# Two-layer streaming encoder on one core: gate products in one block for each attention unit, of 24, 24, 12 and 12 matmuls in turn

## What is computed

```python
z = x @ w_in[l]                      # -> q_A, k_A, v_A, c_q, c_kv, k_rope
y_a = swa(...)                       # mixer A: banded attention, 8 heads of 64, window 128, sinks, bias
y_b = mla(...)                       # mixer B: latent attention, 8 heads, over 512 rows or a cache of 512 + 16
g = sigmoid(x @ w_gate + b_gate)     # 1024 -> 2048: the gate products
h = g[:, :D] * (y_a @ w_proj_a) + g[:, D:] * (y_b @ w_proj_b)
x = LN1(alpha * x + h @ w_out)
x = LN2(alpha * x + ConvGLU(x))
```

## Time and profile before

| | |
|---|---|
| median of 3 runs | 1992.0 us (1989.5 to 1996.69) |
| the profiled execution | 1990.17 us, its span 1988.4 us |
| TensorE busy (matmuls) | 1896.4 us, 95% |
| weight loads on TensorE | 1790.4 us, 90% |
| DVE, ACT, GpSimd busy | 51%, 34%, 28% |
| mean granted clock of TensorE | 0.982 of full speed |
| instructions in the profile | 32255 |
| attention of layer 0, from the first gate matmul to the last values | 151.8 to 390.4 us |
| attention of layer 1 | from 1131.4 us |

### The profile page before, as it was taken

How to read it: one execution, slowest core, us unless ns; L and a number is a source line. 1 busy time by engine, 2 the same in 40 slices (tenths; PEclk the granted TensorE clock), 3 DMA queues, 4 the chain that set the end, 5 groups by cost and what they waited for, 6 DMA issues and landing times.

```text
span 1988.4 us, 32255 instructions
## 1 busy us (share of the span) xinstructions
PE 1896.4 (95%) x12626; PEld 1790.4 (90%) x12626; DVE 1023.7 (51%) x1589; ACT 667.6 (34%) x1372; POOL 566.3 (28%) x252
## 2 busy tenths in 40 slices
PE   7988999999999999999999889999999999999996
PEld 6876788799899999999988778888998999999996
DVE  3457534447764432443664674445587543334447
ACT  2224333442454312332231343334334442123323
POOL 2421111124143234332322211111332432443331
PEclk9999999999999999999989999999999999999998
DMA  6333222242122122221231412323321221222111
GB/s 176 114 87 116 78 81 98 73 151 86 43 85 84 57 70 94 75 69 53 80 119 54 146 42 90 102 78 110 123 79 43 86 78 64 70 97 72 61 59 65
DMA packets 58800, 169.41 MB, mean 85 GB/s; under 512 B 8120, under 2 KB 26216, under 8 KB 50728
## 3 DMA queue, kind: packets, MB, share of 16 engines
q1 hardware_dynamic: 58696, 167.97, 25.2%
HBM read 149.42 MB, written 18.28 MB: 84 GB/s over the span
## 4 chain that ended last, share of the span: by engine, by line
PE 83%; DVE 6%; issue 4%; ACT 2%; DMA 2%; POOL 2%; SPq 1%; POOLq 0%; ACTq 0%; DVEq 0%
PE ps L1429 58%; PE ps L1661 9%; PE ps L1736 3%; PE ps L1459 2%; PE ps L1587 2%; POOL w_lo L617 2%; PE ps L1564 2%; ACT probs L711 1%; PE ps L1634 1%; PE ps L1573 1%; DVE rms L995 1%; DVE probs L1095 1%; DVE st_mx L1066 1%; DVE probs L1065 1%; PE ps L1571 1%
## 5 line engine op out<-in xcount | busy, mean ns | idle before, releaser
L617 POOL TENSOR_TENSOR w_lo<-w_raw,w_hi 128x1024 fp32r<-128x1024 f32 (+3 forms) x248 | 566.1, 2291 | 1387.1 <-ACT w_hi L668 1376.4
L668 ACT ACTIVATE w_hi<-w_raw 128x1024 fp32r<-128x1024 f32 (+3 forms) x244 | 231.2, 968 | 416.5 <-PE ps L1429 398.2
L1429 PE MATMUL ps<-x_hi,w_hi 128*128 128x320 f32 x1504 | 346.1, 311 | 13.3 <-POOL w_lo L617 13.3
L1429 PE MATMUL ps<-x_lo,w_hi 128*128 128x320 f32 x1504 | 345.0, 311 | 0.0
L1429 PE MATMUL ps<-x_hi,w_lo 128*128 128x320 f32 x1504 | 344.8, 311 | 0.0
L1429 PEld LDWEIGHTS ps<-x_hi,w_hi 128*128 128x128 f32 x1504 | 253.6, 189 | 15.0 <-issue 5.9
L1429 PEld LDWEIGHTS ps<-x_lo,w_hi 128*128 128x128 f32 x1504 | 253.9, 189 | 0.0
L1429 PEld LDWEIGHTS ps<-x_hi,w_lo 128*128 128x128 f32 x1504 | 253.6, 189 | 0.0
L1661 PE MATMUL ps<-x_hi,w_hi 128*128 128x320 f32 x512 | 173.8, 339 | 8.5 <-ACT logits L744 8.3
L1334 DVE TENSOR_SCALAR f_conv<-f_ext,vec 128x656 f32<-128x656 f32 x44 | 67.3, 1529 | 211.1 <-ACT tail L879 209.5
L1661 PE MATMUL ps<-x_hi,w_lo 128*128 128x320 f32 x512 | 159.6, 312 | 0.0
(11 more groups left out here) (238 smaller groups left out, 3173.0 us busy)
## 6 DMA issues: line engine op xcount, KB each, us to landing
w_raw<-in_slabs SPq DMA_DIRECT2D x86, 1024.0 KB, 4.8
w_raw<-in_slabs SPq DMA_DIRECT2D x20, 768.0 KB, 4.0
gate_logits<-logits SPq DMA_DIRECT2D x64, 160.0 KB, 1.8
gates<-gate_logits SPq DMA_DIRECT2D x16, 640.0 KB, 6.5
w_raw<-in_slabs SPq DMA_DIRECT2D x16, 640.0 KB, 3.7
ckvc<-in_ckvc SPq DMA_DIRECT2D x16, 256.0 KB, 2.9
ckvc_t<-in_ckvc_t SPq DMA_DIRECT2D x16, 256.0 KB, 3.0
x_in<-in_x_t SPq DMA_DIRECT2D x4, 640.0 KB, 8.7
```

The lines of the kernel that those rows point to most:

```text
L617: pool.tensor_tensor(w_lo[:, s % 2, c], w_raw[:, s % 2, c], w_hi[:, s % 2, c].bitcast(F32), ALU.subtract).then_inc(wlo_ready, 1)
L668: A(w_hi[:, s % 2, c], w_raw[:, s % 2, c], ACT.Copy).then_inc(whi_ready, 1)
L1429: ins = MM(out_[:, a, :], w, x[:, t, a * HT:(a + 1) * HT], start=t == 0 and w is wh and x is hi, stop=t == tiles - 1 and w is wl)
```

## The change

The gate products of a unit are no longer spread over three places. Behind scores(u+2) and ahead of values(u) stands one block: two halves (24 matmuls, one whole product) in units 0 and 1 of every four, one half (12 matmuls) in units 2 and 3. The number of matmuls is the same, and so is that of halves before units 0, 4, 8 and so on. ACT's `take_gate` always stands behind exps(u+2). `quarter_at_scores` follows the new counts: 48, 54, 64, 72, 80, 90, 100, 108 for the eight caches, before 48, 54, 64, 72, 82, 90, 100, 108.

```diff
 NG = 4 * KD
-assert 2 * NG == 4 + 3 * NU // 2
-
-
-def halves_behind(u, step):
-
-    n = 3 * u + step
-    return [] if n % 2 else [4 + n // 2]
-
-
-def gate_ends(g):
-
-    return divmod(4 * g - 6, 3)
+BLOCKS = (2, 2, 1, 1)
+assert NU % 4 == 0 and 2 * NG == 4 + sum(BLOCKS) * NU // 4
+
+
+def halves_before(u):
+
+    return 4 + sum(BLOCKS) * (u // 4) + sum(BLOCKS[:u % 4])
+
+
+def halves_of(u):
+    return range(halves_before(u), halves_before(u + 1))
 
 
 def quarter_at_scores(u):
-    return 0 if u < 2 else 2 * (4 + (3 * (u - 2) + 2) // 2)
+    return 0 if u < 2 else 2 * halves_before(u - 2)
...
                 for u in range(NU):
                     turned_half(u)
-                    for g in range(NG):
-                        if gate_ends(g) in ((u, 0), (u, 1)):
-                            take_gate(g)
                     if u + 2 < NU:
                         exps(u + 2)
-                    for g in range(NG):
-                        if gate_ends(g) == (u, 2):
-                            take_gate(g)
+                    for h in halves_of(u):
+                        if h % 2 == 1:
+                            take_gate(h // 2)
...
                 for u in range(NU):
                     turn(u)
-                    for h in halves_behind(u, 0):
-                        gate_half(h)
                     if u + 2 < NU:
                         scores(u + 2)
-                    for h in halves_behind(u, 1):
+                    for h in halves_of(u):
                         gate_half(h)
                     values(u)
-                    for h in halves_behind(u, 2):
-                        gate_half(h)
```

## The result

The changed kernel takes 2004.34 us (median of 4 runs, 2001.08 to 2006.23) against 1991.28 beside it: ratio 1.0059, 95% interval 1.0036 to 1.0083. It is slower by some 13 us, and its time lies above the predicted range. The profiled execution took 2003.97 us (span 2002.2), before 1990.17.

A forecast was written before the change was run, and what follows sets the result against it. TensorE, busy 95% of 1988.4 us, was taken as the bound. Per layer +5.1 - 4.25 - 0.6 = +0.25, for two layers +0.5: 1990.7 against 1990.17, at the median's level 1992.5; range 1985 to 2001.

The forecast's parts named there:

- Part 1: Units 0 to 7: waits for ACT's gate take, half clock and DVE meeting GpSimd cost +5.1 us a layer.
- Rival B: Unit 1's stall loses the clock and GpSimd holds DVE: +3.4 us a layer, 1999.3 us; chance 0.28.
- main case: The summed forecast, with unit 1's wait keeping the clock: 1992.5 us, own range 1987 to 1997; chance 0.47.
- Part 2: Wait ahead of unit 17's scores shrinks to 1.35 us and its half clock goes: -4.25 us a layer.
- rival D: Clock still falls at unit 17 among small fp32 steps: 3.1 us a layer stays, 1998.7 us; chance 0.12.
- Part 3: Ends of gate matmul blocks: fewer starts, but every block now ends ahead of values; -0.6 us a layer.
- Part 4: Copies of turned probabilities, gate takes, weights and logit stores stay covered by TensorE's work, no new waits: zero.

The follow-up runs named there:

- e7: Changed kernel with 12 extra fp32r matmuls filling TensorE's waits in each of units 1, 4 and 6; 1993.30 us, ratio 1.0014.
- e4: Kernel before the change, with SP issuing the load of cache 0 ahead of the gate weight load; 1980.57 us, ratio 0.9952.
- e8: Kernel before the change, TensorE's order untouched, but ACT takes every gate product behind exps(u+2); 2039.27 us, ratio 1.0240.
- e1: Changed kernel with SP issuing the load of cache 0 ahead of the gate weight load; 1993.17 us, ratio 1.0014.
- e5: Changed kernel with gate products taken ahead of exps(u+2), weights' high part made later, and cache 0 loaded ahead of gate weights; 1976.62 us, ratio 0.9924.
- e9: Changed kernel with 9 extra fp32r matmuls filling the wait ahead of unit 17's scores; 1998.38 us, ratio 1.0036.
- e10: Changed kernel with 11 small fp32 transposes filling the wait ahead of unit 17's scores; 1995.00 us, ratio 1.0021.
- e11: e5 with more blocks of 24 gate matmuls in units 0 to 7 and blocks of 12 in the last four units; 1971.36 us, ratio 0.9902.
- e12_again: Changed kernel, unedited, profiled once more; 2001.47 us in one run.
- e3: Changed kernel with ACT taking gate products ahead of exps(u+2) and making the gate weights' high part behind its next turned copy; 1988.79 us, ratio 0.9990.

## Why the prediction failed, step by step

**Part 1, the mechanism: right.** The three waits came where they were worked out: 2.25 (forecast 2.25), 2.96 and 3.24 (3.25), 1.58 and 2.53 (2.85). They cost by the collision of DVE and GpSimd, +2.65 and +2.43 with the clock kept (e7) against +2.6. With the clock: +4.41 in layer 0 against +5.1. That this came near is in part luck: the forecast had the clock fall behind units 4 and 6, worth 0.8 and 1.7 us. It fell at unit 4 alone, for longer (the block took 6.50 instead of 3.71), while unit 6's wait, 1.58 instead of 2.85, kept it. In layer 1 it was +7.82, which is the next point.

**Rival B, given 0.28: it happened, in one of the two layers.** The main case had unit 1's wait of 2.25 keep the clock. It did in layer 0; in layer 1 a wait of 2.23 lost it, the block took 5.32 us, and one turn of the loop took 10.2, 3.7 more than 6.57 (forecast 3.4). Unit 4's wait of 3.24 then kept the clock, so B came partly in place of the later loss, 2.7 above the forecast. That both layers must do the same, and that a length which kept the clock once keeps it always, were assumptions that no row carried: in the changed order unit 1's wait of 2.23 to 2.26 us kept the clock in 4 of the 11 stages traced and lost it in 7.

**Part 2, the step that failed most.** The idle was right: 1.42 and 1.38 against 1.35. "Idle of 1.35 is below the 1.51 to 1.95 that kept the clock, so this goes" was wrong, and the price put on it, 3.1 us, was right (43.65 against 40.57). This is rival D, given 0.12. The 1.51 to 1.95 came from another place, and length alone doesn't decide. Even at that place it was no rule: unit 1's wait in the old order, 1.93 to 1.96 us, kept the clock in both layers of the kernel before and in one of e4, and lost it in the other of e4 and in both of e8. At unit 17 the record has no exception: in the seven executions traced (of six kernels) whose unit 17 waited 1.28 to 2.49 us, the half clock followed in all 14 cases, and in the six kernels e1, e4, e5, e9, e10 and e11, where it waited 0.21 or less, in none. D gave two layers 6.2; measured against the forecast it is 3.5 in layer 0, and 4.7 plus 2.1 in units 16 to 19 of layer 1, where the half clock lasted 13.65 us. D's mechanism was thus right, and the reason named for it, small fp32 steps that don't keep the clock up, is not borne out: such steps in place of the idle kept it (e10).

**Part 3: mis-sized.** Forecast -0.6 a layer; from unit 16 on, where no wait or half clock disturbs it in layer 0, the two kernels take 135.07 and 135.15 us. And e1 against e4, both without the wait, has units 8 to 15 at 38.90 against 38.66. It is zero to slightly positive: the starts saved are paid back ahead of the values. In units 20 to 39 of layer 0, from the first gate matmul to what follows, a lone 12 took 1.84 to 1.86 us ahead of transposes or scores and 2.01 to 2.05 ahead of values; a block of 24, now always ahead of values, takes 3.80. The term was mis-sized by having 1.95 for 12 ahead of values.

**Part 4: right in layer 0, not in layer 1.** No new wait of values for turned copies in layer 0. In layer 1 one of 1.36 us appeared in unit 3, behind the delayed loop. It goes with B: of the 16 stages traced with the blocks and the late take, it stands, with 1.35 or 1.36 us, in the 7 that lost the clock at unit 1, and in none of the other 9.

The sum: +0.5 forecast for two layers; part 2 adds 3.5 and 6.8, part 1 takes 0.7 off layer 0 and adds 2.7 to layer 1, part 3 adds 1.3. That is 14.1, as measured.

Two things stay open. One is why unit 1's wait loses the clock in one layer and not in the other. Neither the code nor the length decides it: in layer 0 the two executions of the changed kernel and those of e1, e9 and e10 run the same program on TensorE up to the transposes of unit 15, and the three whose first scores stood at 150.53, 151.12 and 151.16 us kept the clock behind unit 1's 2.25 us, the one at 149.21 lost it there, and the one at 149.03 lost it a unit earlier. So in layer 0 the loss goes with where the whole stage stood in time (in layer 1 the starts alone don't sort the cases). The Trainium skill (TensorE: Matmul & The Clock Gate, Part 1) says that the chip's look at TensorE's activity runs freely, so that where it falls against a kernel's work varies; these rows agree, and the repeat of all five places in e12_again doesn't tell against it, since its first scores stood within 0.7 us of those of the first execution in both layers. That this is the cause no run shows. The other is why waits as long in units 1 to 5 often keep the clock and those at unit 17 never did; filling it with either kind of work shows that the idle is needed for the loss, and not what else is.

## What to carry to other kernels

Where several products share one bank, ask in which place of the other engine's order the bank is given back: moving the release ahead of the long exponentials and the load that was waited for ahead of the one that was not gave 27.7 us over the changed kernel and 15 over the one before, more than either order of the matmuls that was tried (13 us slower, and 5 faster on top of both repairs). Cost a wait of TensorE at its length plus a half-clock stretch with a chance of its own. That a wait of this length has kept its clock in a trace, be it at the same place, is no promise: here the same wait of the same code kept it in one execution and lost it in another. Take away the wait, or fill it. And where a delay of half a microsecond decides whether two engines meet, sum the case with the meeting for each layer by itself.

## What the runs showed of the hardware

- Granted clock, 2.4 or 1.2 GHz, against the idle of TensorE ahead of it, at the places that the argument rests on, in both layers of every trace that has the wait unfilled. "Fell" means that a half-clock stretch began during the wait or within 2.4 us behind it. Old order is that of the kernel before, new order that of the changed one:

| wait ahead of | idle, us | clock kept | fell to 1.2 GHz |
|---|---|---|---|
| scores of unit 17 | 1.28 to 1.67 | 0 | 8 |
| scores of unit 17 | 2.23 to 2.49 | 0 | 6 |
| values of unit 4 and gate matmuls of unit 5, old order | 1.51 to 1.53 | 7 | 0 |
| values of units 3, 4 and 6, early take (e3, e5, e11) | 1.35 to 1.49 | 10 | 0 |
| gate matmuls of unit 1, old order | 1.93 to 1.96 | 3 | 3 |
| the same, new order | 2.23 to 2.26 | 4 | 7 |
| gate matmuls of unit 4, new order | 2.94 to 3.03 | 0 | 7 |
| the same | 3.23 or 3.24 | 3 | 4 |
| gate matmuls of unit 6, new order | 1.57 or 1.58 | 4 | 0 |
| the same | 2.17 to 2.53 | 0 | 8 |

- Shorter waits could lose it too: in e8_before_take_last it fell behind 0.95 us in unit 14 in both layers, and stayed behind 2.59 us in unit 4 in both.
- The half clock behind unit 17's wait lasted 3.41, 6.83, 10.24 or 13.65 us; at one wait of one kernel 13.65 in one execution and 6.83 in the other, TensorE being busy throughout.
- 11 small fp32 transposes, 1.36 us in all, put into unit 17's wait kept the clock as well as 9 fp32r matmuls of 1.56 us, in both layers of one traced execution each.
- A DVE instruction on four columns with two inputs from SBUF (0.15 us alone) took 2.40 us beside a GpSimd instruction that began 0.02 us before it and ran 2.40. In the trace it is an addition of two SBUF tiles; the Trainium skill (GPSIMD Engine Reference, Specifications) names two SBUF inputs on VectorE as a case of contention, and the trace agrees, with the whole of GpSimd's duration as the price here, though DVE's operand is only four columns wide.
